# The last gate step as two steps of 256 columns, with the multiplications around it reordered and some buffers 32 bytes further on

## What is computed

```python
attn = forgetting_attention(q, k, v, f_logit + b_f[i])     # 8 heads x 64
conv = gb * causal_depthwise_conv(gc_in * xc, conv_w[i])   # 512 channels
y_br = einsum('nbsc,ncd->nbsd', stack([attn, conv]), w_branch[i])
x = x + sum(sigmoid([g_attn, g_conv]) * y_br) @ w_out[i]
x = x + peer(rmsnorm(x, g_ffn[i]), ...)                    # 128^2 experts
ple_gate = sigmoid(rmsnorm(x, g_ple[i]) @ w_ple_gate[i])
x = x + ple_gate * (p[i] @ w_ple_proj[i])
return rmsnorm(x, g_final)
```

## Time and profile before

| | us |
|---|---|
| median of 3 runs | 1789.17 (1788.63 to 1789.33) |
| the profiled execution | 1790.26 |
| its span, from first to last instruction | 1788.5 |
| TensorE busy in it | 1768.7 (99%) |
| VectorE / ScalarE / GpSimd busy | 1090.7 / 679.1 / 914.5 |
| mean granted TensorE clock | 0.999 of 2.4 GHz |

### The profile page before, as it was taken

The page is one execution under the profiler, slowest core; times in us unless marked ns, Lnnn a source line. Parts: engine busy times, 40 slices in busy tenths (PEclk is TensorE's granted clock), DMA queues, the critical chain, the costliest instruction groups (busy, mean ns, idle before and its releaser), DMA issues.

```text
span 1788.5 us, 22264 instructions
## 1 busy us (share of the span) xinstructions
PE 1768.7 (99%) x7972; PEld 1450.5 (81%) x7972; DVE 1090.7 (61%) x1945; ACT 679.1 (38%) x1057; POOL 914.5 (51%) x742
## 2 busy tenths in 40 slices
PE   8999999999999999999999999999999999999998
PEld 6777788888888888888888888888888888888886
DVE  7455422458799998952222222235888878888974
ACT  6433322443332223222222222244444444444464
POOL 6323154434337676766666665315666666664200
PEclk9999999999999999999999999999999999999999
DMA  5211133348764444444444444458999999999821
GB/s 205 100 63 60 48 106 98 104 152 320 249 232 154 156 152 138 151 142 148 147 145 145 143 151 131 159 200 281 369 381 364 375 351 366 377 367 382 333 83 47
DMA packets 155565, 360.99 MB, mean 202 GB/s; under 512 B 32064, under 2 KB 73024, under 8 KB 155328
## 3 DMA queue, kind: packets, MB, share of 16 engines
q1 hardware_dynamic: 100976, 257.47, 41.5%
q0 software_dynamic: 34816, 67.41, 10.5%
q10 hardware_dynamic: 19664, 34.70, 5.4%
HBM read 298.44 MB, written 61.01 MB: 201 GB/s over the span
## 4 chain that ended last, share of the span: by engine, by line
PE 97%; ACT 1%; another core or an unknown queue 1%; DMA 0%; DVE 0%; issue 0%; ACTq 0%; DVEq 0%
PE pair L791 38%; PE pair L565 18%; PE pair L567 18%; PE pair L566 18%; PE pair L616 1%; PE pair L675 1%; PE pair L695 1%; PE pair L757 1%; PE pair L665 1%; PE pair L800 0%; PE pair L839 0%; DMA x<-xT 0%; DMA ka<-ncum 0%; ACT wh L940 0%
## 5 line engine op out<-in xcount | busy, mean ns | idle before, releaser
L1448 DVE TENSOR_TENSOR wl<-raw,wh 128x1024 fp32r<-128x1024 f32 x254 | 309.3, 1220 | 343.9 <-ACT wh L940 323.4
L519 POOL DMA_INDIRECT gates<-gate_val,gate_at x384 | 412.5, 1074 | 205.0 <-issue 103.6
L791 PE MATMUL pair<-hh,wh 128*128 128x512 f32 x1024 | 399.0, 390 | 1.8 <-ACT gout L1151 1.0
L791 PE MATMUL pair<-hh,wl 128*128 128x512 f32 x1024 | 398.4, 389 | 0.2 <-issue 0.2
L791 PE MATMUL pair<-hl,wh 128*128 128x512 f32 x1024 | 398.5, 389 | 0.0
L940 ACT ACTIVATE wh<-raw 128x1024 fp32r<-128x1024 f32 x339 | 356.5, 1054 | 107.6 <-PE pair L567 97.5
L502 POOL TENSOR_TENSOR wl<-raw,wh 128x1024 fp32r<-128x1024 f32 x85 | 206.1, 2431 | 313.9 <-ACT wh L940 313.9
L565 PE MATMUL pair<-wh,act_h 128*128 128x512 f32 x768 | 299.0, 389 | 0.0
L566 PE MATMUL pair<-wl,act_h 128*128 128x512 f32 x768 | 298.8, 389 | 0.0
L567 PE MATMUL pair<-wh,act_l 128*128 128x512 f32 x768 | 298.8, 389 | 0.0
L1151 ACT ACTIVATE gout<-pair 128x512 f32<-128x512 f32 x128 | 76.4, 597 | 489.1 <-PE pair L791 453.2
(11 more groups left out here) (247 smaller groups left out, 1935.3 us busy)
## 6 DMA issues: line engine op xcount, KB each, us to landing
raw<-stream SPq DMA_DIRECT2D x338, 512.0 KB
score_dram<-gout ACTq DMA_DIRECT2D x128, 256.0 KB
gates<-zeros SPq DMA_DIRECT2D x48, 512.0 KB, 5.8
score_in<-score_dram SPq DMA_DIRECT2D x128, 192.0 KB
gate<-gates SPq DMA_DIRECT2D x128, 192.0 KB
gates<-gate_val,gate_at POOLq DMA_INDIRECT x384
x<-xT SPq DMA_DIRECT2D x4, 512.0 KB, 6.6
picked<-score_dram,score_at POOLq DMA_INDIRECT x128
```

The source lines that it names most:

```text
L519: nc.gpsimd.indirect_dma_start(gate_list, bass.IndirectOffsetOnAxis(ap=gate_at[:, r, k:k + 1], axis=0), gate_val[:, r, k:k + 1], None).the ...
L791: last = nc.tensor.matmul(psum[u % 2][:], w(weights, U_DENSE + u, c), halves[:, c, :], start=c == 0 and which == 0, stop=c == DC - 1 and w ...
L1448: nc.vector.tensor_tensor(wl[:, n % SL, :], raw[:, n % RAW, :], wh[:, n % SL, :].bitcast(F32), ALU.subtract).then_inc(low_own, 1)
```

## The change

The eight gate steps become a list, `STEPS`, whose last entry is split: the last tile's second half is done as columns 0 to 255 (into bank 7) and columns 256 to 511 (into bank 6), 24 multiplications of 256 columns each. Sigmoid, multiplication, addition and square sum of that half are split likewise. The sum of squares of the first quarter is added to `bias3` by one more small VectorE instruction, and the last one goes alone into the square root. Of `out(2)`, the first half now stands ahead of `scale3(3)`. `token` grows from 16 to 48 bytes, of which 16 are used as before; a new `last_sum` takes 32 bytes further on. So `attn_h`, `attn_l`, `conv_h`, `conv_l`, `ka`, `gout` and their neighbours move by 32 bytes: `attn_h` from byte 159,648 of a partition, which is 32 over a multiple of 128, to 159,680, 64 over one (all four results alike). Everything from `spare` on moves by 64: `xh` from 64 over a multiple of 128 to a multiple, `act_h` and `act_l` from a multiple to 64 over. `hh`, `hl`, `wh` and `wl` stay on multiples of 128.

```diff
+STEPS = [(half, i, 0, T) for half in range(2) for i in range(TT)]
+STEPS[-1:] = [(1, TT - 1, 0, T // 2), (1, TT - 1, T // 2, T)]
...
-        token = sb("token", [P, TT], F32)
+        token = sb("token", [P, 3 * TT], F32)
...
-        spare = sb("spare", [P, 2 * TT + 1], F32)
+        last_sum = sb("last_sum", [P, 1], F32)
+        spare = sb("spare", [P, 2 * TT + 2], F32)
...
-            def ple_gate(half, i):
+            def ple_gate(step):
+                half, i, first, end = STEPS[step]
...
-                bank = psum[6 + step % 2].rearrange("p (j w) -> p j w", j=4)
+                bank = psum[6 + step % 2][:, 0:end - first].rearrange("p (j w) -> p j w", w=P)
+                js = slice(first // P, end // P)
...
-            for half in range(2):
-                for i in range(TT):
-                    ple_gate(half, i)
-                    if half == 1 and i == 2:
-                        turn3(0)
-                        turn3(1)
+            for step in range(len(STEPS)):
+                ple_gate(step)
+                if step == TT + 2:
+                    turn3(0)
+                    turn3(1)
             turn3(2)
             turn3(3)
...
-                nc.scalar.activation(sg[:, step % 2, :], psum[6 + step % 2], ACT.Sigmoid).then_inc(sg_ready, 1)
+                nc.scalar.activation(sg[:, step % 2, 0:end - first], psum[6 + step % 2][:, 0:end - first], ACT.Sigmoid).then_inc(sg_ready, 1)
...
+                total = ssq3[:, half, i:i + 1] if step < len(STEPS) - 1 else last_sum[:]
+                nc.scalar.activation(squares[:, 0:end - first], xt[END_ORDER[i]][:, half * T + first:half * T + end], ACT.Square,
+                                     accum_out=total).then_inc(squared3, 1)
...
+            act.wait_ge(squared3, len(STEPS))
+            act.wait_ge(bias_ready, 2)
+            nc.scalar.activation(std3[:, TT - 1:TT], last_sum[:], ACT.Sqrt, bias=bias3[:, TT - 1:TT], scale=1.0 / D).then_inc(std3_ready, 1)
...
+                change = upd[:, step % 2, 0:end - first]
+                nc.vector.tensor_tensor(change, sg[:, step % 2, 0:end - first], emb[half][:, tile, first:end], ALU.mult).then_inc(upd_ready, 1)
...
+                elif step == TT + 3:
+                    dve.wait_ge(squared3, step + 1)
+                    nc.vector.scalar_tensor_tensor(out=bias3[:, i:i + 1], in0=ssq3[:, 1, i:i + 1], scalar=1.0 / D,
+                                                   in1=bias3[:, i:i + 1], op0=ALU.mult, op1=ALU.add).then_inc(bias_ready, 1)
+            out(2, (0,))
             scale3(3)
-            out(2)
+            out(2, (1,))
             out(3)
```

More of the change, by code:

```diff
@@ L893, in _ @@
                     turn2(3)
-            def ple_gate(half, i):
-                tile, step = END_ORDER[i], TT * half + i
+            def ple_gate(step):
+                half, i, first, end = STEPS[step]
+                tile = END_ORDER[i]
                 cols = slice(tile * P, (tile + 1) * P)
@@ L908, in ple_gate @@
                     last = three(bank, hh[:, c, cols], hl[:, c, cols],
-                                 weights(wh, n, 2, c % 2, "p (j k w) -> p k j w"), weights(wl, n, 2, c % 2, "p (j k w) -> p k j w"),
+                                 weights(wh, n, 2, c % 2, "p (j k w) -> p k j w")[:, js], weights(wl, n, 2, c % 2, "p (j k w) -> p k j w")[:, js],
                                  c == 0, c == DC - 1)
@@ L1258, in std3_of @@
                                      scale=1.0 / D).then_inc(std3_ready, 1)
-            for step in range(2 * TT):
-                half, i = divmod(step, TT)
+            for step, (half, i, first, end) in enumerate(STEPS):
                 nc.scalar.activation(spare[:, step:step + 1], eps[:], ACT.Sigmoid)
@@ L1265, in _ @@
                     act.wait_ge(upd_ready, step - 1)
-                nc.scalar.activation(sg[:, step % 2, :], psum[6 + step % 2], ACT.Sigmoid).then_inc(sg_ready, 1)
-                if step == 2 * TT - 1:
-                    nc.scalar.activation(spare[:, 2 * TT:], eps[:], ACT.Sqrt)
+                nc.scalar.activation(sg[:, step % 2, 0:end - first], psum[6 + step % 2][:, 0:end - first], ACT.Sigmoid).then_inc(sg_ready, 1)
+                if step == len(STEPS) - 1:
+                    nc.scalar.activation(spare[:, step + 1:step + 2], eps[:], ACT.Sqrt)
                 act.wait_ge(x3_ready, step + 1)
@@ L1277, in _ @@
                     std3_of(1)
-                elif step > TT + 1:
+                elif step == TT + 2:
                     std3_of(i)
+            act.wait_ge(squared3, len(STEPS))
+            act.wait_ge(bias_ready, 2)
+            nc.scalar.activation(std3[:, TT - 1:TT], last_sum[:], ACT.Sqrt, bias=bias3[:, TT - 1:TT], scale=1.0 / D).then_inc(std3_ready, 1)
             act.wait_ge(rstd3_ready, TT)
@@ L1669, in scale3, with out @@
                 nc.vector.tensor_scalar(part, part, std3[:, i:i + 1], None, ALU.mult).then_inc(left3, 1)
-            def out(i):
-                for half in range(2):
+            def out(i, halves=(0, 1)):
+                for half in halves:
                     k = 2 * i + half
@@ L1687, in _ @@
                     dve.wait_ge(x3_ready, step - 1)
-                nc.vector.tensor_tensor(upd[:, step % 2, :], sg[:, step % 2, :], emb[half][:, tile, :], ALU.mult).then_inc(upd_ready, 1)
+                change = upd[:, step % 2, 0:end - first]
+                nc.vector.tensor_tensor(change, sg[:, step % 2, 0:end - first], emb[half][:, tile, first:end], ALU.mult).then_inc(upd_ready, 1)
                 dve.wait_ge(upd_ready, step + 1)
-                part = xt[tile][:, half * T:(half + 1) * T]
-                nc.vector.tensor_tensor(part, part, upd[:, step % 2, :], ALU.add).then_inc(x3_ready, 1)
+                part = xt[tile][:, half * T + first:half * T + end]
+                nc.vector.tensor_tensor(part, part, change, ALU.add).then_inc(x3_ready, 1)
                 if step == TT - 1:
```

4 lines of the change are left out of this document (1 added, 3 removed).

## The result

| | before | after |
|---|---|---|
| median, 6 runs each | 1788.95 (1788.38 to 1791.60) | **1803.08** (1802.92 to 1803.57) |
| ratio, 95% interval | | 1.0078 (1.0065 to 1.0091) |
| span of the profiled execution | 1788.5 | 1801.8 |
| TensorE busy | 1768.7 | 1783.5 |

What follows compares the result with a forecast made beforehand. The prediction took TensorE to bound the kernel (97% of the span), with the store transfers as the queue at the very end. Savings of 0.83 + 0.22 + 0.39 = 1.4 us from 1789.17 gave 1787.8, range 1786.5 to 1790.5.

Steps and rivals of the forecast that it cites:

- part one: Moved buffers: a multiplication's pace depends on its moving operand's place against a multiple of 128; 0.83 and 0.22 us less.
- Merge, -0.83 forecast: Merge's 8 passes, 24 multiplications moving `conv_*` and `attn_*`: from 0.2338 to 0.2295 each, 0.83 us less.
- `xh`, -0.22 forecast: `xh` units, 3 of 24 multiplications: on a multiple of 128, from 0.2295 to 0.2264 each, 0.22 us less.
- Values, 0 forecast: Value multiplications: the forecast sum had no term for them; standing farther apart than the `hh` stream would prove it wrong.
- Rival 4: Weights `act_h`, `act_l` off a multiple of 128 cost 0.0031 in each of 2304 multiplications: 7.1 us, 1794.9; chance 0.04.
- The end, -0.39 forecast: Behind the last gate step: stores are the queue, an earlier `out(2)` store relieves it; 0.39 us less.
- rival 3: Last gate step: weight loads bind at 256 columns, 0.188 each; 1.2 slower, 1790.4; chance 0.10.
- The first half's wait for `out(1)`: The end: the split step's first `upd` waits until VectorE finishes `out(1)` at 1778.19.
- the square root 0.46 later: The end: root forecast at 1781.91 instead of 1781.38, the scaled row 0.53 later.
- the half of `out(2)` in the gap: The end: first half of `out(2)` fits VectorE's gap before the reciprocal, about 1780.8 to 1781.45, its store issued at 1781.47.
- The bound for a lower clock: The end: last transposes at 1.2 GHz, the eighth 0.9 later, the end about 0.35 later than now.
- a rival of no effect: Moved buffers: the place is not the cause, only the end's 0.4 is left, 1788.8; chance 0.15.

Runs made afterwards that it cites:

- e2: Kernel before with only the places changed (`token` of 48 bytes, unused `last_sum`), old end kept: 1807.43, ratio 1.0088.
- e5: Kernel before with `act_h` and `act_l` 256 bytes on and `xh`, `xl` 192 bytes on: 1788.76 against 1788.63, ratio 1.0003.
- e7: Kernel before with `act_h` and `act_l` 192 bytes on: one run, 1794.30 against 1788.63.
- e3: Changed kernel with 64 unused bytes ahead of `gate`, `act_h` and `act_l` again on a multiple of 128: 1803.86, ratio 1.0076 to the kernel before.
- e4: Kernel before with 64 unused bytes ahead of `wh`, moving `wh`, `wl` and all behind them but not `hh`, `hl`: 1815.67, ratio 1.0136.
- e9: Places of e8, last gate step undivided, only the first half of `out(2)` ahead of `scale3(3)`: 1789.04 against 1792.27 for the kernel before, ratio 0.9987.
- e10: Places of e8, last gate step split, `out(2)` whole behind `scale3(3)`: one run, 1791.85 against 1792.27 for the kernel before.
- e1: Kernel before with the changed end (split and reordered `out(2)`), every buffer in its old place: 1792.05 against 1791.50, ratio 1.0008.
- e8: Changed end; against the kernel before, merge results 32 bytes back, `xh`, `xl` 192 on, `act` unmoved, all in step: 1786.52 against 1788.63, ratio 0.9984.
- e6: Kernel before with 64 unused bytes between `act_h` and `act_l`, moving `act_l` alone: one run, 1799.08 against 1788.63.
- e11: Kernel before with `act_h` 64 bytes on and `act_l` 256 bytes on: one run, 1800.62 against 1792.27.

## Why the prediction was wrong

**The step that failed is part one's "What differs is the moving operand's place".** Three sets of operands were compared, and all three were moved over the same `wh` and `wl`. With the stationary side fixed, a place and a distance to it can't be told apart, and I wrote down the place. The stream in which the change moves the stationary side and leaves the moving one alone, 2304 multiplications and the longest after the scores, was therefore costed at nothing. By the distance all three rows of before still hold, and so do e2 to e5 and e7.

Term by term:

- **Merge, -0.83 forecast, -0.64 measured.** The step from 0.2338 to 0.2295 came (0.2296), since `attn` and `conv` went to the distance that `xh` had. Over all eight passes the 12 that move `attn` reach a mean of 229 ns, the 12 that move `conv` only 231.4, through single longer steps.
- **`xh`, -0.22 forecast, +0.21 measured.** Wrong sign, for the failed step: 64 bytes further it stood on a multiple of 128, but half a period from its weights.
- **Values, 0 forecast, +14.89 measured.** Rival 4 named this place and this operand, and its mechanism as worded ("weights off a multiple cost") fell in e3 and e4. It had two numbers wrong. Its price, 0.0031 each, was that of +64; the change makes -64, and that costs 0.0067. Its chance was 0.04, kept low by the row of `gout` loads, 0.191 beside 0.188, and by "a load has slack". After shows loads of 188 in a stream that lost 6.7 ns a step: durations of loads were no evidence on this at all. With 0.0022 as that rival's own threshold for a loss over 0.2%, it deserved more than any rival about the end.
- **The end, -0.39 forecast, -0.44 measured.** The mechanism held. The first step of 256 columns takes 0.20, the others stand 0.120 apart (1787.49 to 1787.85 are three), against 0.115 taken and 0.137 as the point where rival 3 decides. So the gate's last multiplication starts at +5.71 instead of +5.33, with nobody waiting for it: the second sigmoid comes at +6.76. The first half's wait for `out(1)`, the square root 0.46 later (0.53 forecast) and the half of `out(2)` in the gap came as written. What the text only half said: all the gain is the reorder's (-0.81 in e9), and the split costs 0.45 (e10): its square root is later, and no store is issued earlier for it.
- **The bound for a lower clock**, "the end about 0.35 later than now", was too dark: e1 had it, and its end was 0.06 earlier than before's. The eight transposes lost 0.73 (0.9 forecast), and the end was 0.4 later than e8's, since the transfers cover a part of it.

For the places the Trainium skill, "SBUF — State Buffer", section "Operand start alignment", keeps to what may be addressed. It was quoted for a rival of no effect, and the rule it gives isn't contradicted: every place here was allowed. Closer to the cause is the Trainium skill, "TensorE: Matmul & The Clock Gate", section "Step-by-step: what each phase is for": the moving operand and the weight loads have read ports of their own, and loading the next tile takes no bandwidth from the running multiplication. The runs show something that this doesn't cover. A stream whose two operands stand -64 bytes apart modulo 256 takes 233.4 ns a step, and 226.7 in step, and in e4 both operands of the values 64 bytes further on changed nothing. It would fit that the two reads meet somewhere, but no run shows where, nor that it is bandwidth that they share: the law is measured, its mechanism isn't.

## What to carry to other kernels

Before a buffer is added, grown or dropped, list the places of every TensorE stream's moving and stationary operand behind it, modulo 256, and keep their difference at 0 by padding: here 64 bytes that nothing uses cost 0.9% (e2), and the right pads gave 0.09% (1.68 of the 2.15 us of e8). If a pace is read off streams that share one operand, the other operand's share in it is unknown; look for a stream that varies it, or give the rival that it matters a fair chance, weighted by how many instructions hang on it. At an end that is bound by a queue of stores, move the multiplication and the store of a tile that is ready into an idle gap, and don't split a step for an earlier start unless the wait ahead of its consumer is gone.

## What was not expected of the hardware

- The pace of fp32r multiplications of 512 columns, each with its own load, depends on the distance between the operands: in means of whole streams 226.7 ns at 0 or 256 bytes, 229 at +64, 233.3 at +32, 232.4 at 128, 233.4 at -64. Other distances weren't measured.
- In a stream that mixes distances the prices don't add (13.4, 13.4 and 20 ns a triple for one, two and three off). Steps can be uneven where all three have one distance (226, 229 and 232 at +64).
- The clock of the last eight transposes differed between executions with the same work ahead of them. TensorE had idled 3.07 us (before's end) or about 3.25 (the split ones) each time. In before, after, e2, e7 and e8 all steps but the first were 0.11 us (0.8 from first to last start, 2.4 GHz), with one of 0.13 at the end of e2's; in e1, e5, e6, e10 and e11 all but the first were 0.21 (1.55, 1.2 GHz); in e3, e4 and e9 the clock fell among the eight. Windows around them, before with a mean granted clock of 1.00 and e1 with 0.50:

```profile
1782.40:1784.20 1.80, 1.09 (x8) 0.85 (x8) 1.80 (x4) 0.22 (x1) 0.00 (x0) 1.00 0.14 42
```

```profile
1782.40:1786.00 3.60, 1.97 (x8) 1.57 (x8) 2.37 (x4) 0.62 (x1) 0.00 (x0) 0.50 0.56 167
```

In before the clock fell as well, but behind the transposes: it is at 0.50 from 1784.4 us on. With before's end the slower clock cost nothing, with the changed one 0.4 us (e1 against e8).
